# First layer, second prompt tile: later key rows and first value rows of the expert mixer fetched in turn, inside the sample's second half of heads

## What is computed

```python
def block(xt):                                   # a block of tokens, D = 1024
    q = (xt @ wq).reshape(PEER_BLOCK, PEER_HEADS, 2, PEER_HALF)
    s = jnp.einsum('thpk,hpnk->thpn', q, subkeys)
    ...                                          # top 16 of each half, top 16 of their sums
    expert = ...                                 # 8 heads x 16 = 128 experts for each token
    gate = jax.nn.softmax(sc, axis=-1)
    ue = jnp.take(u, expert, axis=0)             # key rows: 128 rows of 1024 for each token
    act = jax.nn.gelu(jnp.einsum('thed,td->the', ue, xt))
    ve = jnp.take(v, expert, axis=0)             # value rows: 128 rows of 1024 for each token
    return jnp.einsum('the,thed->td', gate * act, ve)
...
x = x + gt1 * mixer(hm)                          # RWKV-7 or GLA
x = x + gt2 * peer(hc)
```

## Time and profile before

| | |
|---|---|
| median of three runs | 2942.13 us |
| the profiled execution: time, span | 2945.39 us, 2943.5 us |
| PE busy | 1921.0 us (65%) |
| DVE busy | 1594.7 us (54%) |
| POOL busy | 1323.4 us (45%) |
| bytes moved by DMA | 841.78 MB, 604.05 MB of them by POOL's fetches |
| mean rate | 286 GB/s |

### The profile page before, as it was taken

How to read it: one execution, slowest core, us unless ns; L and a number is a source line. 1 busy time by engine, 2 the same in 40 slices (tenths; PEclk the granted TensorE clock), 3 DMA queues, 4 the chain that set the end, 5 groups by cost and what they waited for, 6 DMA issues and landing times.

```text
span 2943.5 us, 26768 instructions
## 1 busy us (share of the span) xinstructions
PE 1921.0 (65%) x10173; PEld 1231.3 (42%) x10173; DVE 1594.7 (54%) x2987; ACT 280.3 (10%) x442; POOL 1323.4 (45%) x1160
## 2 busy tenths in 40 slices
PE   5879857837968776657577758678257764453533
PEld 2469523327945435445245227363135433350100
DVE  4253376566752826967412146865961738766033
ACT  1111000020110010010100110001100000000000
POOL 0000012543543555655334235556754675467774
PEclk8989979968789987767798888889568986776876
DMA  8430586964679897767999878789878998899998
GB/s 275 172 130 2 189 308 202 362 238 137 202 266 348 302 325 254 242 217 235 331 355 347 315 253 322 273 281 399 294 275 340 406 386 310 279 353 371 409 409 325
DMA packets 303482, 841.78 MB, mean 286 GB/s; under 512 B 46062, under 2 KB 57246, under 8 KB 303356
## 3 DMA queue, kind: packets, MB, share of 16 engines
q0 software_dynamic: 165888, 604.05, 56.1%
q1 hardware_dynamic: 126900, 231.65, 22.3%
q10 hardware_dynamic: 10568, 4.38, 0.6%
HBM read 829.68 MB, written 10.31 MB: 285 GB/s over the span
## 4 chain that ended last, share of the span: by engine, by line
PE 30%; DVE 24%; DMA 21%; POOL 12%; issue 7%; ACT 3%; PEld 1%; SPq 0%; ACTq 0%; DVEq 0%; PEldq 0%; POOLq 0%
PE psum L1920 28%; POOL arena L721 9%; DVE arena L1125 9%; DVE arena L1105 6%; DMA arena<-in_peer_v,idx_v 6%; POOL wring L721 3%; DMA wring<-in_ada_w 3%; DMA wring<-in_gla_w_in 3%; DMA wring<-in_rw_w_rkv 2%; DMA hc<-in_peer_v,idx_v 2%; DMA wring<-in_peer_wq 1%; PE psum L1938 1%; DVE hT L1105 1%; DMA out<-arena 1%; DMA wring<-in_peer_v,idx_u 1%
## 5 line engine op out<-in xcount | busy, mean ns | idle before, releaser
L721 POOL DMA_INDIRECT arena<-in_peer_u,idx_u x560 | 740.9, 1323 | 1062.1 <-DVE acts L1125 492.7
L1920 PE MATMUL psum<-arena 128*32 128x512 f32 (+6 forms) x3662 | 610.2, 557 | 447.8 <-DMA arena<-in_peer_v,idx_v 170.5
L1125 DVE CUSTOM_DVE_ANT_0 arena<-arena,hc 128x1024 f32<-128x1024 f32 x544 | 644.1, 1224 | 90.6 <-DMA arena<-in_peer_u,idx_u 64.5
L721 POOL DMA_INDIRECT arena<-in_peer_v,idx_v x428 | 422.1, 986 | 461.4 <-PE psum L1920 340.7
L1920 PEld LDWEIGHTS psum<-arena 128*32 128x32 f32 (+2 forms) x3662 | 323.5, 170 | 665.4 <-issue 477.8
L1920 PE MATMUL psum<-pick,ident 128*128 128x256 f32 x1090 | 272.7, 405 | 47.2 <-DVEq L1376 39.2
L1920 PEld LDWEIGHTS psum<-pick,ident 128*128 128x128 f32 x1090 | 215.3, 203 | 132.6 <-issue 54.0
L1920 PE MATMUL psum<-wring,arena 128*32 128x512 f32 (+3 forms) x728 | 213.9, 663 | 77.8 <-DMA wring<-in_peer_v,idx_v 43.0
L1920 PE MATMUL psum<-hT,wring 128*128 128x128 f32 (+3 forms) x1824 | 237.9, 293 | 17.0 <-ACT arena L767 6.3
L1920 PEld LDWEIGHTS psum<-hT,wring 128*128 128x128 f32 (+1 forms) x1824 | 225.7, 198 | 40.0 <-issue 21.9
L1920 PE MATMUL psum<-wring,hT 128*128 128x512 f32 (+1 forms) x480 | 192.2, 560 | 13.5 <-DMA wring<-in_gla_w_in 10.2
(11 more groups left out here) (231 smaller groups left out, 1789.1 us busy)
## 6 DMA issues: line engine op xcount, KB each, us to landing
wring<-in_ada_w SPq DMA_DIRECT2D x24, 2048.0 KB
wring<-in_peer_wq SPq DMA_DIRECT2D x24, 2048.0 KB
wring<-in_rw_w_rkv SPq DMA_DIRECT2D x12, 2048.0 KB
wring<-in_gla_w_in SPq DMA_DIRECT2D x12, 2048.0 KB
wring<-in_rw_wo SPq DMA_DIRECT2D x6, 2048.0 KB
wring<-in_gla_wo SPq DMA_DIRECT2D x6, 2048.0 KB
vring<-mod_d SPq DMA_DIRECT2D x22, 512.0 KB
arena<-in_peer_u,idx_u POOLq DMA_INDIRECT x560, 6.2
```

Source lines behind the costliest of these rows:

```text
L721: pool.indirect_dma_start(slot(s, n), None, v_rows if side else u_rows, bass.IndirectOffsetOnAxis(index, 0)).then_inc(rows_landed[s], 16)
L1125: dve.tensor_tensor_reduce(slot(s, n), slot(s, n), hidden(li, t), 1.0, 0.0, MUL, ADD, acts[:, (3 * li + t) % 2, col:col + 1]).then_inc(row ...
L1920: return nc.tensor.matmul(out, lhsT, rhs, start=start, stop=stop)
```

## The change

Tile 1 of layer 0 is entered in `MINGLED`. `round_at` then gives key rounds 16 to 31 and value rounds 0 to 15 places in turn, and `gather` on POOL issues them so: key round 16, value round 0, key round 17, value round 1, and so on. Since places alternate between the two groups, the key rounds use group 0 and the value rounds use group 1 as long as they alternate. In the second half of the sample's heads DVE serves five key rows at each `fill()` and at no other place (`paired`), and PE serves 1.25 value rounds ahead of each product for DVE and at no other place. The 16 rounds that are left (16 to 31) are opened where all 32 were opened.

```diff
-MINGLED = ()
+MINGLED = ((0, 1),)
...
-            RATES = {"mix": 14, "core1": 1.9, "core2": 4.0, "enter": 6, "gla": 2.6, "out": 7}
+            RATES = {"mix": 14, "core1": 1.9, "core2": 4.0, "core3": 5.0, "enter": 6, "gla": 2.6, "out": 7}
...
                     if hh == 0:
-                        open_rows(0, 1, 64, 64, RATES["core2"])
+                        open_rows(0, 1, 64, 64, RATES["core3"], True)
...
-            VALUE_RATES = {"out": 0.5, "gla": 0.5, "core2": 0.8}
+            VALUE_RATES = {"out": 0.5, "gla": 0.5, "core3": 1.25}
...
+                    if hh:
+                        rest_values()
                     fan_weights(0, 1, hh)
+                    if hh == 0:
+                        open_values(0, 1, VALUE_RATES["core3"], 16, 0, True)
                 if sample:
-                    open_values(0, 1, VALUE_RATES["out"])
+                    open_values(0, 1, VALUE_RATES["out"], 16, 16)
```

## The result

| | before | changed |
|---|---|---|
| median | 2943.47 us (2941.88 to 2962.33) | 3028.06 us (3024.16 to 3035.32) |
| ratio to before | 1 | 1.026 (95%: 1.0226 to 1.0293) |
| profiled execution, span | 2945.39, 2943.5 us | 3024.16, 3022.3 us |
| second half of heads (second turn's start to `fan_weights`) | 152.8 us | 271.0 us |
| from there to GLA's first projection | 167.1 us | 173.8 us |

The change makes the kernel slower by 2.6%, some 77 us by the ratio (67 to 86 by its interval; the medians lie 84.6 apart); 2970 us had been forecast, with 3006 as the upper end. So the direction holds and the size does not. The four stretches of the two profiled executions add up to +78.0 us (118.2 + 6.7 - 25.3 - 21.6), and the rest of the program to +0.8; the two executions differ by 78.8.

The account below looks back on a forecast made before the run. DVE's work paces the second half of heads, with DMA to spare; value rows hold PE in GLA. 2945.4 + 88 - 60 = 2973.4 us for the profiled execution, 2970 for the median, range 2930 to 3006.

Parts of the forecast that it names:

- What is saved in GLA: GLA's projections and `gla(0)`: without the 16 value rounds and their waits, 60 us saved, bounds 50 to 77.
- one weight block: GLA's projections: the sixth weight block, asked for after ACT raised the gates, still keeps PE waiting 4 us.
- a level: `gla(0)`: each of six levels takes 3.9 us instead of 6.5, giving back 16 us.
- The stretch between: From 1417 to 1584 us: same rounds and weights at the same 349 GB/s, costed at nothing.
- The turn: Second half of heads: 3.73 us of fetches, 6.0 landing, 1.92 round on PE, 11.6 us a value round; bounds 10.0 to 14.0.
- the forecast of 88: Second half of heads: 35 + 2 + 17 + 2 + 32 us added, 12 turns exposed; bounds 69 to 117.
- sixth product: Second half of heads, drain at 1316.00: turn hidden by DVE's own chain but for the round on PE, +2 us.
- state loads and the eighth product: Second half of heads: loads cover round 7; rounds 8 and 9 stand ahead of the eighth product, +17 us.
- last four: Second half of heads: rounds 11 to 15 stand ahead of the last four products, five turns, +32 us.
- the one of long turns: Rival 3: longer PE waits, lower clock and delayed POOL fetches give +117 - 50 = +67, 3009 us; chance 0.17.
- Rows in time: Rival 1, second half of heads: landed rounds cost only 1.92 us each, +31 against -60, 2913 us; chance 0.12.
- The rule weighed against the rows: Landing of a 512 KB fetch: 2.0 us plus bytes at 436 GB/s, 3.2 us; turn 8.8 us, additions about 55 us.

Follow-up runs that it names:

- held key rows: Changed kernel with POOL's fetches of the first layer's 8 sample key rows held until PE has done GLA's projections; ratio 1.023 to before (third group added 1.0127).
- short rounds: Changed kernel with value rounds 1 to 15 of tile 1's first layer making only 64 of 1024 product columns, all fetches kept; ratio 1.0184 to before.
- idle products: Changed kernel with 16 idle products on PE ahead of each value round in the second half of heads but the first; ratio 1.0232 to before.
- the one that came out even: Kernel before with only value rounds 0 to 3 moved ahead, into a third group of slots and idle places on PE; ratio 1.0017 to before.
- half rows: Changed kernel with value rounds 0 to 15 of tile 1's first layer fetching half of each row; ratio 1.017 to before (1.0088 with a third group).

## Why the prediction was right in direction and wrong in size

1. **What is saved in GLA: 60 forecast, 46.9 found (25.3 + 21.6).** The waits for value rows went, as said. Two steps were too large. I let one weight block be 4 us late; it was 10.1 us late, since with the value rounds gone POOL's slots are empty and the sample's key rows are fetched at once, 4.2 MB beside the block. The runs with held key rows confirm it: there the block is 4.45 us late, near the 4 that I had. And I took a level at 3.9 us from the one that had waited for nothing; that one ran between value rounds, at a granted clock of 0.85. Without them PE idles between levels, its clock is 0.57 (0.59 in the run that leaves the rounds out), a product takes 2.08 us, and a level 4.56 us: over seven levels 4.6 us.
2. **The stretch between: nothing forecast, 6.7 us found.** The other kernels that moved all 16 rounds have 166 to 176 us there, so this is not told from scatter.
3. **The turn: 11.6 us forecast, 14.07 found.** This is the step that failed. By the means of the five turns in attention, landing is 6.1 us (6.0 forecast) and the four fetches are 4.15 us (3.73 forecast, since some take longer than 0.94). The third part is the one that was mis-sized: 1.92 us for the round, against 3.8 us from its start to the next fetch. I had a round at half the clock, 3.64 us, and with it a turn of 14.0 as the upper bound, and set it aside because the clock lay between its levels *before*. But the turn makes its own clock: PE stands 7 to 11 us ahead of each round, and over these five turns the granted clock was 0.65 (0.75 in attention before). The turns ahead of the later products are like these: 13.9 and 13.7 us from round 7 (1386.67) to round 9 (1414.17), and 13.7 in the mean from round 11 (1453.08) to round 15 (1507.88). 2.4 us by 12 turns would be 29 of the 30 us that the half is over the forecast of 88, a sum from attention's turn alone. The run with short rounds shows the same part from the other side: 2.4 us less in a turn. The run with idle products shows it only in part, 0.8 us in a turn and no gain in time.
4. **DVE's part: nothing forecast, 8 us found** in the run of it alone. I had priced the eight last rows, served earlier, and not the five in a row ahead of each drain. How much of the 8 remains where PE waits for value rows anyway was not told apart; the turns alone, at attention's length, already fill the gap.
5. **Where it lies.** Attention +48.5 (forecast 35), sixth product +0.5 (2), state loads and the eighth product +25.8 (17), ninth +3.8 (2), last four +41.9 (32), and behind the last drain -2.4 (0), where DVE's last eight rows had stood. Of the +25.8, 3.9 us are no turn: the state loads took longer, 23.2 us from the first of their transposes on PE (1361.80) to the last (1385.00), instead of 19.3. The 12 exposed turns, and which drain pays for how many, were right; PE waited exactly 12 times for value rows.
6. **The rivals.** The time fell to the one of long turns (3009, at 0.17), whose +117 for the half is the 118 found; its 50 for GLA was 3 too much, and the stretch between adds 6.7. "Rows in time" could have been excluded by one more line of arithmetic: it asked for a turn below some 6.5 us, and a turn holds eight fetches, a key and a value round, which at 0.94 + 0.30 us take POOL 9.9 us. All misses went the same way: 13 us less saved, 7 in the stretch between and 30 more in the half make the 50 us from the 28 forecast to the 78 found.
7. **The rule weighed against the rows** (the Trainium skill, "DMA: Bandwidth & Descriptors", "Anatomy of one DMA — SWDGE (gpsimd) path") gave 3.2 us for a landing; the rows after show 5.5 us in the middle and 4.2 at the least, so the rows were the better guide. For half of the bytes it gives an estimate of 2.6 us, and the run shows 3.8.

## What to carry to other kernels

Before two streams of gathers are made to share a ring of slots, work out the turn of one stream on its share (release, fetches, landing, and the use at the clock that this very wait leaves), and the time that the issuing engine needs for all fetches of the stage; the free share of DMA tells neither. What is moved out of a stage also takes with it what it held back: here the fetches that full slots had kept from colliding with weights, and the clock that the moved products had kept up. No move here paid; the one that came out even had slots of its own and places that were idle on PE.

## What the runs showed of the hardware that was not expected

- An indirect fetch of 128 rows costs POOL 0.94 us and 0.30 us to the next, 1.24 us, with whole and with half rows alike; so back to back such fetches of 524 KB bring 420 GB/s at most, less here, because some of them take up to 1.99 us. In the half of heads of the kernel before, 32 of 64 fetches took over 1.3 us, and 30 of these lie beside a row product of DVE (L1125) for more than 0.2 us; of the 32 short ones 6 do. In the half of the changed kernel it is 24 of 26 long ones and 20 of 102 short ones. The Trainium skill, "SBUF — State Buffer", "SBUF: two separate sides", tells of DVE operations that lock GpSimd out of a shared pair of ports, so that it cannot write the descriptors of its DMAs. The longer fetches agree with it in kind; that the row product takes that lock, no run here shows.
- Taking 16 value rounds away lowered the granted clock in `gla(0)` from 0.85 to 0.57, and the products of the levels, which nobody had touched, took 2.08 us instead of 1.06.
